# Five feed-forward parts whose rows and weights start at other remainders modulo 128 bytes in SBUF

## The chip, the cores and the metric

The kernel runs on 1 core of one Trainium2 chip, as one launch. The metric is the device time of that core in microseconds (us). The kernel before was timed twice.

## The reference, cut to what matters

The reference is a network of 1024 features and 512 tokens, in float32. Its layers hold five feed-forward parts (two around a recurrent mixer, two around a spatial gating mixer, one behind a last block with attention, a state space branch, a gated linear branch and cross attention). Each part is the same computation with its own weights, here for d = 1024 and f = 2816:

```python
def rms_norm(x, g):
    y = x * rsqrt(mean(x * x, axis=-1) + 1e-6)
    return y * g

def swiglu(x, w_in, w_out):          # w_in [1024, 2*2816], w_out [2816, 1024]
    g, u = split(x @ w_in, 2, axis=-1)
    return (silu(g) * u) @ w_out

h = h + 0.5 * swiglu(rms_norm(h, gain), w_in, w_out)   # four parts; the fifth without the 0.5
```

Between the parts stand the mixers and the last block. The change leaves what they compute and their code as it is, but for the names of the tiles that hold their normed input.

## The kernel before, in words

All arrays are stored with 128 features on the partitions and 512 tokens along the free dimension. A product in float32 is made of three matmuls in the format float32r: every operand is split into a high and a low half (`xg_hi`, `xg_lo` for the rows, `w_hi`, `w_lo` for the weights), and `three_passes` (L457) multiplies high by high, high by low and low by high into one PSUM bank. **Rows** are here the moving operand (the activations, 512 or 256 columns a matmul); **weights** are the stationary operand (128 columns, loaded by a separate LDWEIGHTS).

Weights come from HBM into `w_stage`, a ring of four slots of 1024 float32 each. ScalarE (ACT) writes the high half of a slot into `w_hi` (L424), GpSimd (POOL) the low half into `w_lo` (L448, L455, L803). The loads are issued by the SP queue. Every matrix of the program goes through this ring.

A feed-forward part `i` (`pe_ffn`, L709) has two stages:

- **Up**, with the rows `xg_hi`, `xg_lo` (the normed input). The first and the last pairs of weight slots are multiplied plainly: 8 tiles of the contraction, three passes, 512 columns each (`project_unit`, L464). All between go in **blocks** (`step`, L732): a 2 by 2 block product made with seven products instead of eight. One `step` has seven products of 4 tiles by 3 passes, 84 matmuls of 256 columns (`product`, L712, matmuls at L716 to L718). Three of the seven take their rows from `xg_hi`, `xg_lo` and their weights from the ring (36 matmuls). One takes its rows from `xsum`, sums of rows, and its weights from the ring (12). Three take `xsum` and sums of weights, `s1_w`, `s2_w`, `s3_w` (36). Part 0 has 16 steps, each other part 18.
- **Down**, with the rows `h_hi`, `h_lo` (22 tiles) and the weights from the ring: 8 outputs of 22 tiles by 3 passes, 528 matmuls of 512 columns.

Where a tile lies in SBUF is written by hand. `place` (L149) gives a tile the next free address or the one in `at`. In the kernel before, `x_res`, the ring and all tiles placed after them start at multiples of 2048 bytes, and those placed at `work + n * KB` at multiples of 1024; so the first byte of every high and low half is at remainder 0 modulo 128. The tiles of `k` within them are 2048 bytes apart (1024 in `xsum`), the 128 weight columns of one matmul 512 bytes. One exception matters here: `xsum` lies at `work + 64`, remainder 64. In the notation used below, rows at r and weights at w means the remainders of their start addresses modulo 128.

Order on the engines is fixed by the program text and by semaphores. On TensorE all work of the five parts is in one queue; ACT, DVE and POOL make the sums, the splits and the SwiGLU products beside it.

## Time and profile before

| What | Value |
|---|---|
| Time, median of 2 runs | 2818.24 us (2817.14 and 2819.35) |
| Profiled execution: span, first to last instruction | 2817.5 us |
| TensorE (PE) busy | 2790.9 us, 99% of the span |
| Weight loads (PEld) busy | 2391.3 us, 85% |
| DVE / ACT / POOL busy | 59% / 48% / 56% |
| Mean granted TensorE clock | 0.999 |
| Moved from HBM | 263.09 MB, 94 GB/s |

The page gives the profiled execution's span and no separate time for it. The span lies between the two timed runs, so it is taken as that execution's own time too, and a sum made against it can be held against the median as it is.

How to read the rows: a matmul's duration in the trace (the mean ns of a group) runs from its start until its last result, and neighbours overlap, because matmuls are pipelined. What a matmul costs in a dense stretch is the distance from its start to the start of the next, which is read from a timeline or from a count in a window.

### The profile page before, as it was taken

What the parts mean: (1) busy time and instruction counts of PE and PEld (TensorE: products, weight loads), DVE (VectorE), ACT (ScalarE), POOL (GpSimd) and SP (SyncE); (2) the same over time, 40 slices, a digit from 0 to 9 for tenths busy, and PEclk for the clock granted to TensorE, in tenths of its full rate; (3) what the DMA queues carried; (4) which work ended last, traced back from release to release, by engine and by line L of the source; (5) the groups of instructions that cost most, each with busy time, mean ns of one, the idle gap of its engine ahead of it and who ended that gap; (6) DMA issues with size and microseconds to landing.
All of it is one profiled execution on the core that took longest, in us unless ns stands there. A gap on an engine that the chain in (4) does not pass through costs nothing.

```text
span 2817.5 us, 45558 instructions
## 1 busy us (share of the span) xinstructions
PE 2790.9 (99%) x16386; PEld 2391.3 (85%) x16386; DVE 1657.6 (59%) x2703; ACT 1346.4 (48%) x2076; POOL 1571.1 (56%) x872
## 2 busy tenths in 40 slices
PE   8999999999999999999999999999999999999999
PEld 6998877899889998888999886665688888799987
DVE  6777147677616774135777416579788464477730
ACT  5554257555425554243555334557444444455531
POOL 6775445677547774444777443158633373367743
PEclk9999999999999999999999999999999999999999
DMA  3234322232332233332223332112222342123332
GB/s 136 105 104 115 103 82 82 91 104 104 111 99 90 104 109 105 100 106 89 91 104 120 101 94 77 53 53 66 71 89 70 103 149 75 53 103 107 109 98 77
DMA packets 80685, 267.91 MB, mean 95 GB/s; under 512 B 11168, under 2 KB 13216, under 8 KB 80560
## 3 DMA queue, kind: packets, MB, share of 16 engines
q1 hardware_dynamic: 77904, 262.01, 28.4%
q10 hardware_dynamic: 2656, 4.26, 0.5%
q8 instruction: 74, 1.21, 0.2%
q14 instruction: 51, 0.42, 0.0%
HBM read 263.09 MB, written 2.10 MB: 94 GB/s over the span
## 4 chain that ended last, share of the span: by engine, by line
PE 94%; DVE 3%; ACT 1%; issue 1%; DMA 0%; POOL 0%; ACTq 0%; SPq 0%; DVEq 0%
PE bank L460 17%; PE bank L462 17%; PE bank L461 17%; PE bank L716 10%; PE bank L718 10%; PE bank L717 10%; PE bank L547 1%; PE bank L548 1%; PE bank L549 1%; PE bank L1635 1%; PE bank L2047 1%; PE bank L2915 1%; PE bank L2647 0%; PE bank L2056 0%; PE bank L2627 0%
## 5 line engine op out<-in xcount | busy, mean ns | idle before, releaser
L448 POOL TENSOR_TENSOR w_lo<-w_stage,w_hi 128x1024 fp32r<-128x1024 f32 (+1 forms) x228 | 535.2, 2353 | 714.0 <-ACT w_hi L424 713.5
L424 ACT ACTIVATE w_hi<-w_stage 128x1024 fp32r<-128x1024 f32 (+1 forms) x412 | 421.0, 1027 | 367.2 <-PE bank L462 303.5
L803 POOL TENSOR_TENSOR w_lo<-w_stage,w_hi 128x1024 fp32r<-128x1024 f32 (+1 forms) x176 | 327.3, 1859 | 202.1 <-ACT w_hi L424 202.1
L460 PE MATMUL bank<-xg_hi,w_hi 128*128 128x512 f32 x976 | 396.2, 406 | 5.0 <-DVE h_raw L1063 3.8
L461 PE MATMUL bank<-xg_lo,w_hi 128*128 128x512 f32 x976 | 381.2, 391 | 0.0
L462 PE MATMUL bank<-xg_hi,w_lo 128*128 128x512 f32 x976 | 381.2, 391 | 0.0
L455 POOL TENSOR_TENSOR w_lo<-w_stage,w_hi 128x1024 fp32r<-128x1024 f32 (+1 forms) x96 | 234.9, 2453 | 261.7 <-ACT w_hi L424 217.3
L460 PE MATMUL bank<-h_hi,w_hi 128*128 128x512 f32 x880 | 342.3, 389 | 0.0
L461 PE MATMUL bank<-h_lo,w_hi 128*128 128x512 f32 x880 | 342.3, 389 | 0.0
L462 PE MATMUL bank<-h_hi,w_lo 128*128 128x512 f32 x880 | 342.3, 389 | 0.0
L718 PE MATMUL bank<-xg_hi,w_lo 128*128 128x256 f32 x1056 | 299.2, 283 | 0.0
L716 PE MATMUL bank<-xg_hi,w_hi 128*128 128x256 f32 x1056 | 298.9, 283 | 0.0
L717 PE MATMUL bank<-xg_lo,w_hi 128*128 128x256 f32 x1056 | 298.8, 283 | 0.0
L716 PE MATMUL bank<-xsum,s_w 128*128 128x256 f32 x1056 | 296.1, 280 | 0.0
L718 PE MATMUL bank<-xsum,s_w 128*128 128x256 f32 x1056 | 294.6, 279 | 0.0
L717 PE MATMUL bank<-xsum,s_w 128*128 128x256 f32 x1056 | 294.6, 279 | 0.0
L1136 DVE SCALAR_TENSOR_TENSOR x_res<-bank,x_res 128x512 f32 x64 | 44.0, 687 | 400.9 <-PE bank L462 400.9
L460 PEld LDWEIGHTS bank<-xg_hi,w_hi 128*128 128x128 f32 x976 | 183.6, 188 | 72.5 <-issue 34.5
L1028 DVE TENSOR_TENSOR s_w<-bank,s_w 128x512 fp32r<-128x512 f32 x176 | 121.7, 691 | 190.4 <-ACT s_w L933 190.4
L461 PEld LDWEIGHTS bank<-xg_lo,w_hi 128*128 128x128 f32 x976 | 183.9, 188 | 40.5 <-issue 4.8
L462 PEld LDWEIGHTS bank<-xg_hi,w_lo 128*128 128x128 f32 x976 | 183.6, 188 | 39.7
L716 PEld LDWEIGHTS bank<-xg_hi,w_hi 128*128 128x128 f32 x1056 | 202.4, 192 | 0.2
(530 smaller groups left out, 6599.0 us busy)
## 6 DMA issues: line engine op xcount, KB each, us to landing
w_stage<-w_up SPq DMA_DIRECT2D x220, 512.0 KB, 4.2
w_stage<-w_down SPq DMA_DIRECT2D x80, 512.0 KB, 3.5
w_stage<-merge SPq DMA_DIRECT2D x36, 512.0 KB, 3.4
w_stage<-w_down SPq DMA_DIRECT2D x40, 384.0 KB, 3.2
...
```

What stands on the lines that cost most here:

```text
L424: act.activation(w_hi[:, r, 0:w], w_stage[:, r, 0:w], ACT.Copy).then_inc(w_hi_ready, 1)
L448: pool.tensor_tensor(w_lo[:, r, 0:w], w_stage[:, r, 0:w], f32(w_hi[:, r, 0:w]), ALU.subtract).then_inc(w_lo_ready, 1)
L455: pool.tensor_tensor(w_lo[:, r, 0:w], w_stage[:, r, 0:w], f32(w_hi[:, r, 0:w]), ALU.subtract).then_inc(w_lo_ready, 1)
L460: pe.matmul(out, w_hi[:, r, c], hi, start=start, stop=False)
L461: pe.matmul(out, w_hi[:, r, c], lo, start=False, stop=False)
L462: return pe.matmul(out, w_lo[:, r, c], hi, start=False, stop=stop)
L716: pe.matmul(out, wh[:, c], xh[:, k, :], start=k == 0, stop=False)
L717: pe.matmul(out, wh[:, c], xl[:, k, :], start=False, stop=False)
L718: mm = pe.matmul(out, wl[:, c], xh[:, k, :], start=False, stop=k == 3)
L803: pool.tensor_tensor(w_lo[:, r, cs], w_stage[:, r, cs], f32(w_hi[:, r, cs]), ALU.subtract).then_inc(w_lo_ready, 1)
L1028: dve.tensor_tensor(lo, src[:], f32(hi), ALU.subtract).then_inc(wsum_lo_ready, 1)
L1136: dve.scalar_tensor_tensor(tile(x, m), bank[mm % 4][:], scale, tile(x, m), ALU.mult, ALU.add).then_inc(taken, 1)
```

## The change

The change gives tiles of the same contents several homes, and each feed-forward part uses its own:

- `xg_of[q]`: the normed rows, a pair of tiles for each norm `q`, all over the same memory. `xg_lo` moves 128 bytes further from `xg_hi`.
- The ring: each slot of `w_hi` and `w_lo` gets 32 more float32, so a slot is 4224 bytes long and no longer 4096. The block products of part `i` use columns that begin `BLOCK_ASIDE[i]` float32 into the slot, its down stage `DOWN_ASIDE[i]`. All else, the plain products of the up stage included, begins at the slot's start. Slot r therefore starts 128 * r bytes later than in a ring of 4096.
- `xsum_of`, `s12_of`, `s3_of`, `h_of`, `h_raw_of`: the same for the sums and for `h`. The low half of `h` moves 128 bytes further.
- The size given for dynamic DMA scratch in SBUF is set to 1024, which frees room; the layout is up to some 8 KB longer.

In remainders modulo 128 bytes, rows and then weights (before: 0, 0 everywhere, but for `xsum` with 64, 0):

| Part | blocks, `xg` | blocks, `xsum` | down | plain products of up |
|---|---|---|---|---|
| 0 | 0, 64 | 0, 64 | 64, 64 | 0, 0 |
| 1 | 32, 96 | 32, 96 | 32, 32 | 32, 0 |
| 2 | 96, 32 | 96, 32 | 96, 96 | 96, 0 |
| 3 | 0, 32 | 0, 32 | 0, 32 | 0, 0 |
| 4 | 0, 96 | 0, 96 | 0, 96 | 0, 0 |

No instruction is added, taken out or moved: each of the five engines has the same operations in the same order, with the same waits, and only addresses differ. Its core:

```diff
+    XG_REMAINDER = {0: (0, 0), 1: (0, 0), 2: (32, 32), 3: (96, 96), 4: (0, 0), 5: (0, 0), FINAL: (0, 0), 8: (0, 0), 9: (0, 0)}
+    XSUM_REMAINDER = (0, 32, 96, 0, 0)
+    H_REMAINDER = ((64, 64), (32, 32), (96, 96), (0, 0), (0, 0))
+    BLOCK_ASIDE = (16, 24, 8, 8, 24)
+    DOWN_ASIDE = (16, 8, 24, 8, 24)
...
-    xg_hi = place("xg_hi", [P, KD, T], F32R)
-    xg_lo = place("xg_lo", [P, KD, T], F32R)
+    XG_BASE = cursor[0]
+    xg_of = {q: (place(f"xg_hi{q}", [P, KD, T], F32R, at=XG_BASE + high),
+                 place(f"xg_lo{q}", [P, KD, T], F32R, at=XG_BASE + KD * T * 4 + 128 + low)) for q, (high, low) in XG_REMAINDER.items()}
+    cursor[0] += 2 * KD * T * 4 + LINE
     w_stage = place("w_stage", [P, RING, UNIT])
-    w_hi = place("w_hi", [P, RING, UNIT], F32R)
-    w_lo = place("w_lo", [P, RING, UNIT], F32R)
+    ring_hi = place("ring_hi", [P, RING, UNIT + 32], F32R)
+    ring_lo = place("ring_lo", [P, RING, UNIT + 32], F32R)
+    w_hi, w_lo = ring_hi[:, :, 0:UNIT], ring_lo[:, :, 0:UNIT]
+    wb_of = [(ring_hi[:, :, a:a + UNIT], ring_lo[:, :, a:a + UNIT]) for a in BLOCK_ASIDE]
+    wd_of = [(ring_hi[:, :, a:a + UNIT], ring_lo[:, :, a:a + UNIT]) for a in DOWN_ASIDE]
+
+    def ring_of(L):
+        return wd_of[int(L.name[4])] if L.name.startswith("down") else (w_hi, w_lo)
...
-    h_hi = place("h_hi", [P, KF, T], F32R)
-    h_lo = place("h_lo", [P, KF, T], F32R)
+    h_of = [(place(f"h_hi{i}", [P, KF, T], F32R, at=work + high),
+             place(f"h_lo{i}", [P, KF, T], F32R, at=work + KF * T * 4 + 128 + low)) for i, (high, low) in enumerate(H_REMAINDER)]
...
-    xsum = place("xsum", [P, 4, 2, 4, HALF], F32R, at=work + 64)
-    s1_w = place("s1_w", [P, 2, T], F32R, at=work + 33 * KB)
-    s2_w = place("s2_w", [P, 2, T], F32R, at=work + 37 * KB)
+    xsum_of = [place(f"xsum{i}", [P, 4, 2, 4, HALF], F32R, at=work + off) for i, off in enumerate(XSUM_REMAINDER)]
+    s12_of = [(place(f"s1_w{i}", [P, 2, T], F32R, at=work + 32 * KB + 128 + 4 * a),
+               place(f"s2_w{i}", [P, 2, T], F32R, at=work + 36 * KB + 256 + 4 * a)) for i, a in enumerate(BLOCK_ASIDE)]
...
-    def three_passes(pe, out, r, j, hi, lo, start, stop):
+    def three_passes(pe, out, r, j, hi, lo, start, stop, ring=(w_hi, w_lo)):
 
         c = slice(j * P, (j + 1) * P)
-        pe.matmul(out, w_hi[:, r, c], hi, start=start, stop=False)
-        pe.matmul(out, w_hi[:, r, c], lo, start=False, stop=False)
-        return pe.matmul(out, w_lo[:, r, c], hi, start=False, stop=stop)
+        pe.matmul(out, ring[0][:, r, c], hi, start=start, stop=False)
+        pe.matmul(out, ring[0][:, r, c], lo, start=False, stop=False)
+        return pe.matmul(out, ring[1][:, r, c], hi, start=False, stop=stop)
...
     def pe_ffn(pe, i, q):
+        (s1_w, s2_w), s3_w, (wb_hi, wb_lo) = s12_of[i], s3_of[i], wb_of[i]
         U, L = layers[f"up{i}"], layers[f"down{i}"]
+        xg_hi, xg_lo = xg_of[q]
+        h_hi, h_lo = h_of[i]
+        xsum = xsum_of[i]
...
         def w_block(p, row, c):
             cs = slice(c * T, (c + 1) * T)
-            return w_hi[:, 2 * p + row, cs], w_lo[:, 2 * p + row, cs]
+            return wb_hi[:, 2 * p + row, cs], wb_lo[:, 2 * p + row, cs]
...
-                                          k == 0, k == KF - 1)
+                                          k == 0, k == KF - 1, ring_of(L))
```

The other edits pass the same tiles to ACT, DVE and POOL, which write them.

## Rows read from the trace of the kernel before

**Rows 1.** the page, parts 1 and 2: busy time; slices of the span.
```profile
PE 2790.9 (99%) x16386; PEld 2391.3 (85%) x16386; DVE 1657.6 (59%) x2703; ACT 1346.4 (48%) x2076; POOL 1571.1 (56%) x872
...
PEclk9999999999999999999999999999999999999999
```

**Rows 2.** the page, part 4: the chain that ended last.
```profile
PE 94%; DVE 3%; ACT 1%; issue 1%; DMA 0%; POOL 0%; ACTq 0%; SPq 0%; DVEq 0%
PE bank L460 17%; PE bank L462 17%; PE bank L461 17%; PE bank L716 10%; PE bank L718 10%; PE bank L717 10%; PE bank L547 1%; PE bank L548 1%; PE bank L549 1%; PE bank L1635 1%; PE bank L2047 1%; PE bank L2915 1%; PE bank L2647 0%; PE bank L2056 0%; PE bank L2627 0%
```

**Rows 3.** timeline of PE, one step of part 0: start us, us, engine line op names.
```profile
151.18 0.29 PE L716 MATMUL bank<-xg_hi,w_hi 128*128 128x256 f32 x1
...
155.50 0.28 PE L716 MATMUL bank<-xsum,s_w 128*128 128x256 f32 x1
...
161.16 0.29 PE L716 MATMUL bank<-xg_hi,w_hi 128*128 128x256 f32 x1
```

**Rows 4.** groups by form, PE: names, shapes, count, busy us, mean ns, idle before.
```profile
L716 PE MATMUL bank<-xg_hi,w_hi 128*128 128x256 f32 x1056 | 298.9, 283 | 0.0
...
L716 PE MATMUL bank<-xsum,s_w 128*128 128x256 f32 x1056 | 296.1, 280 | 0.0
...
L716 PE MATMUL bank<-xsum,w_hi 128*128 128x256 f32 x352 | 98.5, 280 | 0.0
```

**Rows 5.** groups by form, weight loads (PEld).
```profile
L716 PEld LDWEIGHTS bank<-xg_hi,w_hi 128*128 128x128 f32 x1056 | 202.4, 192 | 0.2
...
L716 PEld LDWEIGHTS bank<-xsum,s_w 128*128 128x128 f32 x1056 | 198.6, 188 | 0.3
...
L460 PEld LDWEIGHTS bank<-h_hi,w_hi 128*128 128x128 f32 x880 | 165.2, 188 | 34.2
```

**Rows 6.** timeline of PE, projection of the memory: 24 matmuls from first to last row.
```profile
2249.17 0.28 PE L460 MATMUL bank<-mem_hi,w_hi 128*128 128x256 f32 x1
...
2252.04 0.28 PE L460 MATMUL bank<-mem_hi,w_hi 128*128 128x256 f32 x1
```

**Rows 7.** windows: PE, PEld, DVE, ACT, POOL busy (instructions), clock, DMA share, GB/s.
```profile
101.00:211.00 110.00, 110.00 (x928) 110.00 (x927) 82.70 (x155) 59.74 (x100) 82.01 (x56) 1.00 0.30 105
248.00:358.00 110.00, 110.00 (x487) 91.09 (x486) 30.22 (x64) 31.76 (x39) 50.88 (x23) 1.00 0.35 103
```

**Rows 8.** timeline of PE, the forget gate, weights 8 columns wide.
```profile
1718.44 0.39 PE L1683 MATMUL bank<-xg_hi,ff_hi 128*8 128x512 f32 x1
...
1719.12 0.40 PE L1683 MATMUL bank<-xg_hi,ff_hi 128*8 128x512 f32 x1
1719.35 0.40 PE L1684 MATMUL bank<-xg_lo,ff_hi 128*8 128x512 f32 x1
1719.59 0.39 PE L1685 MATMUL bank<-xg_hi,ff_lo 128*8 128x512 f32 x1
...
1723.28 0.40 PE L1683 MATMUL bank<-xg_hi,ff_hi 128*8 128x512 f32 x1
```

**Rows 9.** timeline of PE, down stage of part 0: twelve matmuls from first to last row.
```profile
300.03 0.39 PE L460 MATMUL bank<-h_hi,w_hi 128*128 128x512 f32 x1
...
302.75 0.39 PE L460 MATMUL bank<-h_hi,w_hi 128*128 128x512 f32 x1
```

**Rows 10.** groups by form, ACT: a write at remainder 0, one at 64.
```profile
L424 ACT ACTIVATE w_hi<-w_stage 128x1024 fp32r<-128x1024 f32 x368 | 385.1, 1051 | 234.4 <-PE bank L462 170.7 <-PE bank L549 30.7 <-PE bank L718 24.3
...
L871 ACT ACTIVATE xsum<-xsum_f 128x1024 fp32r<-128x1024 f32 x20 | 20.0, 1047 | 0.2
```

**Rows 11.** groups by form, POOL: the same pair.
```profile
L448 POOL TENSOR_TENSOR w_lo<-w_stage,w_hi 128x1024 fp32r<-128x1024 f32 x188 | 460.4, 2454 | 594.1 <-ACT w_hi L424 593.5
...
L807 POOL TENSOR_TENSOR xsum<-xsum_f,xsum 128x1024 fp32r<-128x1024 f32 x20 | 48.6, 2430 | 0.0
```

**Rows 12.** groups by form, PE: down stage, and projections of the other layers.
```profile
L460 PE MATMUL bank<-xg_hi,w_hi 128*128 128x512 f32 x976 | 396.2, 406 | 5.0 <-DVE h_raw L1063 3.8 <-POOL w_lo L455 1.2
...
L460 PE MATMUL bank<-h_hi,w_hi 128*128 128x512 f32 x880 | 342.3, 389 | 0.0
```

More of the change, by code:

```diff
@@ L173, in build @@
     s3_w = place("s3_w", [P, 2, T], F32R, at=cursor[0] - 2 * T * 4)
+    s3_of = [place(f"s3_w{i}", [P, 2, T], F32R, at=cursor[0] - 2 * T * 4 + 4 * a) for i, a in enumerate(BLOCK_ASIDE)]
+    cursor[0] += LINE
     ss = place("ss", [P, T])
@@ L186, in build @@
     KB = 1024
-    h_raw = place("h_raw", [P, KF, T], at=work + KF * T * 4)
-    xsum = place("xsum", [P, 4, 2, 4, HALF], F32R, at=work + 64)
-    s1_w = place("s1_w", [P, 2, T], F32R, at=work + 33 * KB)
-    s2_w = place("s2_w", [P, 2, T], F32R, at=work + 37 * KB)
+    h_raw_of = [place(f"h_raw{i}", [P, KF, T], at=work + KF * T * 4 + 128 + low) for i, (_, low) in enumerate(H_REMAINDER)]
+    xsum_of = [place(f"xsum{i}", [P, 4, 2, 4, HALF], F32R, at=work + off) for i, off in enumerate(XSUM_REMAINDER)]
+    s12_of = [(place(f"s1_w{i}", [P, 2, T], F32R, at=work + 32 * KB + 128 + 4 * a),
+               place(f"s2_w{i}", [P, 2, T], F32R, at=work + 36 * KB + 256 + 4 * a)) for i, a in enumerate(BLOCK_ASIDE)]
     u_add0 = place("u_add0", [P, T], at=work + 41 * KB)
@@ L423, in split_hi @@
             act.wait_ge(unit_used, b * L.per + (L.base + i + 1 - RING))
-        act.activation(w_hi[:, r, 0:w], w_stage[:, r, 0:w], ACT.Copy).then_inc(w_hi_ready, 1)
+        act.activation(ring_of(L)[0][:, r, 0:w], w_stage[:, r, 0:w], ACT.Copy).then_inc(w_hi_ready, 1)
     def act_bodies(act, L, work=None, only=None):
@@ L447, in body @@
                 pool.wait_ge(w_hi_ready, b * L.per + (L.base + i + 1))
-                pool.tensor_tensor(w_lo[:, r, 0:w], w_stage[:, r, 0:w], f32(w_hi[:, r, 0:w]),
+                hi, lo = ring_of(L)
+                pool.tensor_tensor(lo[:, r, 0:w], w_stage[:, r, 0:w], f32(hi[:, r, 0:w]),
                                    ALU.subtract).then_inc(w_lo_ready, 1)
@@ L566, in act_norm_tile @@
     def act_norm_tile(act, q, gain, m, buf):
-        act.activation(tile(xg_hi, m), tile(x, m), ACT.Copy, scale=col(*gain(m))).then_inc(xg_hi_ready, 1)
+        act.activation(tile(xg_of[q][0], m), tile(x, m), ACT.Copy, scale=col(*gain(m))).then_inc(xg_hi_ready, 1)
         act_norm_square(act, q, m, buf)
@@ L792, in pool_up @@
     def pool_up(pool, U, i):
+        xsum = xsum_of[i]
+        (s1_w, s2_w), s3_w, (wb_hi, wb_lo) = s12_of[i], s3_of[i], wb_of[i]
         def plain(b, u):
@@ L870, in act_x_high @@
         act.wait_ge(xsum_done, XSUMS * i + XSUM_COUNT[t])
-        act.activation(xsum[:, t, 0], xsum_f[:, 1 + t], ACT.Copy).then_inc(wsum_hi_ready, 1)
+        act.activation(xsum_of[i][:, t, 0], xsum_f[:, 1 + t], ACT.Copy).then_inc(wsum_hi_ready, 1)
     def act_ffn_entry(act, i, gain):
@@ L900, in act_ffn @@
     def act_ffn(act, i, gain):
+        h_hi, h_raw = h_of[i][0], h_raw_of[i]
+        (s1_w, s2_w), s3_w, (wb_hi, wb_lo) = s12_of[i], s3_of[i], wb_of[i]
         U, L = layers[f"up{i}"], layers[f"down{i}"]
         def row1(b, p):
-            split_hi(act, U, b, 2 * p)
+            r = 2 * p
+            act.wait_ge(w_loaded[r], b * 16 + 16 * (U.base // RING + 1))
+            act.wait_ge(unit_used, b * 4 + (U.base + r + 1 - RING))
+            act.activation(wb_hi[:, r, :], w_stage[:, r, :], ACT.Copy).then_inc(w_hi_ready, 1)
         def row2(b, p):
@@ L909, in row2 @@
             act.wait_ge(unit_used, b * 4 + (U.base + r + 1 - RING))
-            act.activation(w_hi[:, r, T:2 * T], w_stage[:, r, T:2 * T], ACT.Copy).then_inc(w_hi_ready, 1)
+            act.activation(wb_hi[:, r, T:2 * T], w_stage[:, r, T:2 * T], ACT.Copy).then_inc(w_hi_ready, 1)
         def copy21(b, p, n):
@@ L1236, in pe_rec @@
                 pe.wait_ge(gates_sig, 2 * KD)
-            project_unit(pe, R if s < KD else Y, u // 4, u % 4, xg_hi, xg_lo,
+            project_unit(pe, R if s < KD else Y, u // 4, u % 4, *xg_of[q],
                          (xg_lo_ready, split_count(q)) if s == 0 else None, out=y_bank(u) if s >= KD else None)
@@ L1377, in norms_read @@
             pe.wait_ge(col_std, 1)
-        pe_project_tokens(pe, V, xg_hi, xg_lo, norm=norms, ready=(xg_lo_ready, split_count(q)), between=norms_read)
+        pe_project_tokens(pe, V, *xg_of[q], norm=norms, ready=(xg_lo_ready, split_count(q)), between=norms_read)
         def mix(h):
@@ L1390, in pe_sgu @@
         for u in range(KD):
-            project_unit(pe, U, u // 4, u % 4, xg_hi, xg_lo, free=V.rbase + u + 1 if u < 4 else None)
+            project_unit(pe, U, u // 4, u % 4, *xg_of[q], free=V.rbase + u + 1 if u < 4 else None)
             if u == 2:
@@ L1527, in result @@
                 act.wait_ge(taken, m + (L.rbase + 1))
-                act.activation(tile(xg_hi, m), tile(x, m), ACT.Copy, scale=gain12[:, bass.ds(m, 1)]).then_inc(xg_hi_ready, 1)
+                act.activation(tile(xg_of[FINAL][0], m), tile(x, m), ACT.Copy, scale=gain12[:, bass.ds(m, 1)]).then_inc(xg_hi_ready, 1)
                 act.wait_ge(ss_added, m * 2 + ((KD + 1) * FINAL + 2))
@@ L2019, in first_half @@
             half(u, 0)
+        xg_hi, xg_lo = xg_of[FINAL]
         def half(u, part):
@@ L3262, in _ @@
             act.wait_ge(x_in[m // 2], 32)
-            act.activation(xg_hi[:, m, :], x[:, m, :], ACT.Copy, scale=col("ffn1_norm", m)).then_inc(xg_hi_ready, 1)
+            act.activation(xg_of[0][0][:, m, :], x[:, m, :], ACT.Copy, scale=col("ffn1_norm", m)).then_inc(xg_hi_ready, 1)
         split_hi(act, order[0], 0, 1)
```

20 lines of the change are left out of this document (15 added, 5 removed).

## The prediction

> **What bounds the kernel now.** I read the page's first parts first. TensorE (PE) is busy for 2790.9 of 2817.5 us, and its granted clock is at the upper of its two levels, 2.4 GHz, in all slices [rows 1]. The chain that ended last agrees: 94% of it is matmuls, over half of it the 512-column passes of L460 to L462 and 30% the block products of L716 to L718 [rows 2]. So the time is a number of matmuls times the distance from one start to the next, and a change of addresses matters to the end only through that distance, as long as no other engine becomes late.
>
> Then the distances. At 2.4 GHz a matmul of 256 columns streams in 106.7 ns and one of 512 in 213.3 ns. In a step of part 0, the 36 matmuls on `xg` take 155.50 - 151.18 = 4.32 us, **120.0 ns each**; the 48 matmuls on `xsum` behind them take 161.16 - 155.50 = 5.66 us, **117.9 ns each** [rows 3]. The down stage goes at 2.72 us / 12 = **226.7 ns** each [rows 9]; its group has one mean, 389 ns, over all five parts [rows 12], so I take 226.7 for each of them. All of these are 11 to 13 ns above the streaming time.
>
> Why are `xsum` products 2.1 ns faster? The groups show the same shape and form, 283 against 280 ns [rows 4]. The weights are not the reason: `xsum` with weights from the ring has the same 280 ns as with the sums [rows 4]. The steps between tiles are not the reason either: the memory's rows have tiles 1024 bytes apart like `xsum`, but start at remainder 0, and go at 2.87 us / 24 = 119.6 ns [rows 6], the pace of `xg`. What is left is the start: `xsum` is the only one of the three at remainder 64, with its weights at 0. The weight loads tell the same: 192 ns beside rows at 0, 188 ns beside `xsum` [rows 5]. I read it as this: a load and a stream that begin at the same remainder disturb each other by some 4 ns, of which half shows in the distance. With 512 columns the load has twice the time.
>
> **The change part by part.** No instruction comes or goes; five things move.
>
> 1. *Blocks of parts 0 to 2, rows on `xg`.* Rows and weights come to stand 64 apart (0 and 64, 32 and 96, 96 and 32), where they were 0 apart. Steps: 16 + 18 + 18 = 52, of 36 such matmuls, 1872 in all. At 120.0 - 117.9 = 2.1 ns each that is **-3.9 us**. That the distance modulo 128 decides, and not both remainders by themselves, is an assumption; the rows have only 0 with 0 and 64 with 0.
> 2. *Blocks of parts 0 to 2, rows on `xsum`.* 64 apart before and after: **0**.
> 3. *Blocks of parts 3 and 4.* All pairs are now 32 or 96 apart, which no row shows. 36 steps: 1296 matmuls on `xg` (now 120.0) and 1728 on `xsum` (now 117.9). Bounds: all of them at 117.9 gives -1296 x 2.1 = -2.7 us; all at 120.0 gives +1728 x 2.1 = +3.6 us. I take the middle, 118.95 ns for both, since 32 lies between 0 and 64: -1.4 + 1.8 = **+0.4 us**. The far ends are in the rivals.
> 4. *Down stages.* Parts 0 to 2 keep rows and weights together (64, 32, 96): by the assumption of step 1, 0. Parts 3 and 4 have 1056 matmuls with the weights alone at 32 or 96. The nearest row with such weights is the forget gate, whose weights are 8 columns (32 bytes) a tile, so that they start at 0, 32, 64, 96, 128 and so on, with rows at 0. Its first three passes take 0.68 us, 226.7 each; the next 18 take 4.16 us, 231.1 each [rows 8], so +4.4 ns. But these loads are 8 columns wide, not 128. On the other side stands a gain like that of the blocks, -2.1 ns. Between +4.6 and -2.2 us I take **0**: in a down stage a load is recorded with 188 ns like the undisturbed ones [rows 5] beside a matmul of 389 [rows 12], so it has time to spare, and the blocks' 2.1 ns need not show there.
> 5. *Everything else.* The plain products of parts 1 and 2 have rows at 32 and 96 against weights at 0: 2 x 192 = 384 matmuls, 0 in the middle, between -0.8 and +1.7 us by the prices of step 4. The low halves are 128 bytes further and slot r of the ring 128 * r bytes; modulo 128 nothing changes, so 0 (but see the second rival). Sum without the rivals: -3.9 + 0 + 0.4 + 0 + 0 = -3.5 us.
>
> *Cover.* The other engines now read and write at 32, 64 and 96. At 64 that is free: ACT needs 1047 ns into `xsum` and 1051 into the ring for the same size [rows 10], POOL 2430 and 2454 [rows 11]. For 32 and 96 there is no row. In the blocks DVE is busy for 82.7, POOL for 82.0 and ACT for 59.7 of 110 us, and PE for all 110 with 928 matmuls; in the down stage they have at most 50.9 of 110 [rows 7]. A tenth more on all of them would leave POOL at 90 of 110 and PE still ahead. If that cover went, PE's idle time before L716, 0.0 us now [rows 4], would grow, by DVE's and POOL's low halves first, the two with the least room. Should PE get faster by 2% the same room holds. The DMAs land in `w_stage`, whose slots stay as they are.
>
> 2817.5 - 3.5 = 2814.0 us for the profiled execution. Its span lies between the two timed runs, and the median is 0.7 us above it; I predict **2814 us**.
>
> **The rivals.**
>
> *Nothing moves (2818 us).* The `xsum` products are faster for a reason that moves with them, such as what precedes them in the queue. For it: only 2.1 ns are at stake, and no two rows differ in the remainder alone. Against it: the memory's rows. The time is that of before, 2817.5 to 2818. The Trainium skill ("SBUF — State Buffer", Specifications) gives 16-byte cachelines to SBUF as the unit whose crossing costs; 32, 64 and 96 all start such a line, and so by that rule no start here is worse or better than another. The difference between 283 and 280 ns [rows 4] speaks against the rule being the whole story.
>
> *Slower: weights that do not start at a multiple of 256 bytes.* In the forget gate the tile at 128 goes no faster than those at 32 or 96: the 18 passes that take 231.1 each hold it [rows 8]. If it is the weights' start and not their width, the price of 4.4 ns is paid by every 512-column pass whose weights are off such a start. These are all 2640 of the down stages (+11.6 us), and, since slots 1 and 3 of the longer ring now start 128 bytes off, half of the passes of all other projections. L460 to L462 have 976 such groups of three on `xg` alone [rows 12], so about 2930 passes, of which half pay: +6.4 us. With -3.5 us from the forecast's steps this makes 2817.5 + 11.6 + 6.4 - 3.5 = **2832 us**. It decides from the point where the down stage of any part goes above 228 ns; if only weights alone at 32 or 96 pay (parts 3 and 4), it is +4.6 us and 2818.6. Against it: 8-column loads are the only such row, and weights at 0 never show it in a dense stretch.
>
> *More is gained: another distance lets the passes close up.* The 11 to 13 ns above streaming are there in each pass, and nothing in the rows says that 0 and 64 are the only levels. The lower bound is streaming itself. In the down stages of parts 3 and 4 that is -1056 x 13.4 = -14.1 us, **2800 us** with the forecast's -3.5; if the blocks of these parts close up too, another -1296 x 13.3 - 1728 x 11.2 = -36.6 us, 2763 us. For it: 64 apart already took 2.1 ns. Against it: it took only 2.1 of 13.3, and the 8-column loads, which hardly read anything, do not come below 226.7 either [rows 8], so most of the gap does not come from the load beside. The Trainium skill ("TensorE: Matmul & The Clock Gate", Wait — 56ns, not 53.3ns?) gives N / 2.4 + 2.5 ns from start to start for bfloat16; that would be 215.8 ns for 512 columns, and by it the most that the two down stages could gain is 11.5 us. The trace has 226.7 in float32r and no row of it shows that pace.
>
> *The change does not do what it says.* The remainders come from absolute offsets that I worked out from the listing; the base of all is rounded to 128, then to 2048 bytes, in both kernels, so a shift against the table is hardly possible. I give it no share of its own.
>
> **How the numbers follow.** Forecast, 2808 to 2817: 0.50. Nothing moves: 0.17. Slower, 2818.6 to 2832 and somewhat above: 0.18. More is gained, 2763 to 2807: 0.15. The range reaches from the first half of the third rival, 2800, to the full price of the second, 2832, with 2 us on either side for the spread of the runs: **2798 to 2834**; outside are some 0.10 below and 0.06 above. Two per cent, taken as what a measurement of this kernel can tell from no change, is 56 us. Faster by that would need 2762, the whole of the third rival and a little more: 0.03. Slower by that would need 5.5 ns on all of the some 10,000 matmuls of the five parts, 1.2 times the gate's price even where only 256 columns are streamed: 0.02. Within: 0.95.
>
> **What would show it.** In the trace of the changed kernel: (1) start to start of the `xg` block matmuls in parts 0 to 2 at about 117.9 ns, and their weight loads at 188 in place of 192 ns; that fails if they stay at 120. (2) The `xsum` matmuls there unchanged. (3) In parts 3 and 4 both kinds between 117.9 and 120. (4) The down stages at 226.7 in all five parts; above 228 is the second rival, below 222 the third. (5) The projections outside the five parts as before; if they slow down, the ring's longer slots are the cause. (6) PE's idle time before L716's successor still 0. The prediction is wrong in kind if the five parts differ from each other by more than 2 ns a matmul, and if DVE, ACT or POOL appear as what PE waits for.

## The result, and the profile after

The changed kernel takes **2836.56 us** (2835.99 and 2837.13), against 2818.24: a ratio of 1.006, with a 95% interval of 1.0041 to 1.0079. It is slower by 18 us. My 2814 was wrong in sign, and 2836.6 lies above the range, which ended at 2834.

The first parts of the page and the share by engine of the chain that ended last:

```profile
span 2835.3 us, 45558 instructions
...
PE 2809.5 (99%) x16386; PEld 2383.4 (84%) x16386; DVE 1658.5 (58%) x2703; ACT 1345.1 (47%) x2076; POOL 1572.8 (55%) x872
...
PEclk9999999999999999999999999999999999999999
...
PE 95%; DVE 3%; ACT 1%; issue 1%; DMA 0%; POOL 0%; ACTq 0%; SPq 0%; DVEq 0%
```

Against [rows 1, 2] one thing moves: PE is busy 18.6 us longer with the same 16386 matmuls, at the upper clock level in every slice. No other engine's busy time moves by more than 1.7 us, and none is waited for more by over 0.3 us. So what changed is the distance from start to start, and that is what the rest of this text reads. Below it stands for five places of the timeline of PE after: one step of part 0 (answers [rows 3]), the down stage of part 0 and that of part 3, first and last of 528 matmuls each ([rows 9]), and in the layer with rows `m`, which the change did not touch, 21 matmuls in an even slot of the ring and 21 in the odd slot behind it.

```profile
141.00 0.28 PE L739 MATMUL bank<-xg_hi,ring_hi 128*128 128x256 f32 x1
...
145.24 0.28 PE L739 MATMUL bank<-xsum,s_w 128*128 128x256 f32 x1
...
150.80 0.28 PE L739 MATMUL bank<-xg_hi,ring_hi 128*128 128x256 f32 x1
...
243.00 0.39 PE L478 MATMUL bank<-h_hi,ring_hi 128*128 128x512 f32 x1
...
364.77 0.39 PE L480 MATMUL bank<-h_hi,ring_lo 128*128 128x512 f32 x1
...
1570.24 0.40 PE L478 MATMUL bank<-h_hi,ring_hi 128*128 128x512 f32 x1
...
1692.67 0.40 PE L480 MATMUL bank<-h_hi,ring_lo 128*128 128x512 f32 x1
...
2333.77 0.39 PE L478 MATMUL bank<-m_hi,ring_hi 128*128 128x512 f32 x1
...
2338.30 0.40 PE L480 MATMUL bank<-m_hi,ring_lo 128*128 128x512 f32 x1
...
2339.24 0.39 PE L478 MATMUL bank<-m_hi,ring_hi 128*128 128x512 f32 x1
...
2343.89 0.40 PE L480 MATMUL bank<-m_hi,ring_lo 128*128 128x512 f32 x1
```

The block products got faster: 36 on `xg` in 4.24 us, 117.8 ns each, and 48 on `xsum` in 5.56 us, 115.8 ns. The down stages got slower: 121.77 us / 527 = 231.1 ns in part 0, 122.43 / 527 = 232.3 in part 3, where each had 226.7. The layer on `m` is at 4.53 us / 20 = 226.5 ns in the even slot, as before, and at 4.65 / 20 = 232.5 in the odd one. The odd slots begin 128 bytes off a multiple of 256.

Within the down stage of part 0 the two kinds of slot differ the other way round. Its rows are at 64 (high) and 192 (low) modulo 256, its weights at 64 in an even slot and at 192 in an odd one. Three starts, of an even slot with 24 matmuls, an odd one with 18 and the next even one:

```profile
263.69 0.40 PE L478 MATMUL bank<-h_hi,ring_hi 128*128 128x512 f32 x1
...
269.30 0.39 PE L478 MATMUL bank<-h_hi,ring_hi 128*128 128x512 f32 x1
...
273.42 0.40 PE L478 MATMUL bank<-h_hi,ring_hi 128*128 128x512 f32 x1
```

The even slot takes 5.61 us / 24 = 233.8 ns a matmul, the odd one 4.12 / 18 = 228.9. The other slots of this stage have the same two paces, but for the first one, which is even and goes at 229.2.

The groups by form (PE, then weight loads) answer [rows 4, 5, 12]: the load beside `xg` fell from 192 to 188 ns, as forecast, and no idle time came before the block products. The mean of 188 is over all five parts. The window of the blocks holds 945 matmuls in 110 us where there were 928 ([rows 7]).

```profile
L478 PE MATMUL bank<-h_hi,ring_hi 128*128 128x512 f32 x880 | 347.0, 394 | 0.0
...
L739 PE MATMUL bank<-xg_hi,ring_hi 128*128 128x256 f32 x1056 | 296.0, 280 | 0.0
...
L739 PE MATMUL bank<-xsum,s_w 128*128 128x256 f32 x1056 | 294.8, 279 | 0.0
```

```profile
L739 PEld LDWEIGHTS bank<-xg_hi,ring_hi 128*128 128x128 f32 x1056 | 198.4, 188 | 0.2
```

```profile
101.00:211.00 110.00, 110.00 (x945) 110.00 (x944) 84.04 (x157) 59.91 (x102) 83.98 (x58) 1.00 0.30 105
```

The table has this account for every kernel here: the block stages and the down stages of the five parts, each from the start of its first matmul to that of its last, summed, and the rest up to the start of the program's last matmul. The rest holds the other layers, the plain products of the up stages, and the program's start: the first block stage begins 61.1 to 64.5 us into the span, 62.8 before and 64.0 in the change. In that start the granted clock falls to its lower level, 1.2 GHz, for 3.4 us before (from 39.9 us on) and for 6.8 in the change (from 38.3 on). Between 30 and 40 us TensorE was busy for 6.2 and 5.9 of 10 us there; in b1_xglow, where it was busy for 7.4, the clock did not fall. So 1 to 3 us of a difference in the rest can be the start alone.

| Kernel | blocks, us | down, us | rest, us | time, us |
|---|---|---|---|---|
| before | 877.7 | 597.3 | 1338.9 | 2818.2 |
| the change | 868.3 | 610.3 | 1353.1 | 2836.6 |
| a1_slots | 862.0 | 606.3 | 1349.0 | 2822.8 |
| a2_lows | 853.7 | 609.0 | 1350.0 | 2818.1 |
| a3_by256 | 870.4 | 604.9 | 1342.0 | 2822.8 |
| a4_rows0_w64 | 867.9 | 597.3 | 1340.4 | 2811.0 |
| b1_xglow | 853.5 | 597.3 | 1341.3 | 2799.7 |
| b2_map | 864.4 | 606.2 | 1341.5 | 2817.6 |
| c1_xglow192 | 854.2 | 597.5 | 1340.2 | 2797.5 |
| c2_xglow64 | 871.6 | 597.3 | 1344.5 | 2820.7 |
| c3_part1 | 873.0 | 597.3 | 1341.1 | 2816.8 |
| d1_lowmap | 869.4 | 597.4 | 1342.6 | 2814.9 |
| d2_summap | 873.5 | 597.3 | 1341.6 | 2817.9 |

So the change is worth -9.4 us in the blocks, +13.0 in the down stages and +14.2 elsewhere. The times of before, the change, a4, b1, c1 and c2 are medians of several runs, the others one run each; the three columns of stages are always from the one profiled execution. The kernel before, run again beside the experiments, took 2818.5 to 2825.9 us, so a single time is good only to some us. The stages repeat better: the down stages are at 597.3 to 597.5 us in seven of the experiments.

### The profile page after: what moved, and what is told of

Its sections match the earlier page's. It is cut to its first block, busy times and chain, and to the rows that moved or that the text cites. A ratio compares the mean times of both kernels' runs of the same rounds, so it can differ in the third digit from the quotient of the medians.

```text
span 2835.3 us, 45558 instructions
## 1 busy us (share of the span) xinstructions
PE 2809.5 (99%) x16386; PEld 2383.4 (84%) x16386; DVE 1658.5 (58%) x2703; ACT 1345.1 (47%) x2076; POOL 1572.8 (55%) x872
## 4 chain that ended last, share of the span: by engine, by line
PE 95%; DVE 3%; ACT 1%; issue 1%; DMA 0%; POOL 0%; ACTq 0%; SPq 0%; DVEq 0%
PE bank L478 18%; PE bank L480 18%; PE bank L479 18%; PE bank L741 10%; PE bank L740 10%; PE bank L739 10%; PE bank L565 1%; PE bank L566 1%; PE bank L567 1%; PE bank L1669 1%; PE bank L2084 1%; PE bank L2954 1%; PE bank L2686 0%; PE bank L2093 0%; PE bank L2666 0%
## 5 line engine op out<-in xcount | busy, mean ns | idle before, releaser
L466 POOL TENSOR_TENSOR ring_lo<-w_stage,ring_hi 128x1024 fp32r<-128x1024 f32 (+1 forms) x228 | 537.4, 2363 | 732.3 <-ACT ring_hi L441 732.0
L441 ACT ACTIVATE ring_hi<-w_stage 128x1024 fp32r<-128x1024 f32 (+1 forms) x324 | 328.7, 1021 | 377.2 <-PE bank L480 310.8
L828 POOL TENSOR_TENSOR ring_lo<-w_stage,ring_hi 128x1024 fp32r<-128x1024 f32 (+1 forms) x176 | 327.0, 1858 | 197.5 <-ACT ring_hi L934 197.0
L478 PE MATMUL bank<-xg_hi,ring_hi 128*128 128x512 f32 x976 | 400.3, 410 | 5.2 <-DVE h_raw L1095 4.1
L480 PE MATMUL bank<-xg_hi,ring_lo 128*128 128x512 f32 x976 | 384.4, 394 | 0.0
L479 PE MATMUL bank<-xg_lo,ring_hi 128*128 128x512 f32 x976 | 383.6, 393 | 0.0
L473 POOL TENSOR_TENSOR ring_lo<-w_stage,ring_hi 128x1024 fp32r<-128x1024 f32 (+1 forms) x96 | 234.9, 2452 | 263.5 <-ACT ring_hi L441 218.6
L478 PE MATMUL bank<-h_hi,ring_hi 128*128 128x512 f32 x880 | 347.0, 394 | 0.0
L479 PE MATMUL bank<-h_lo,ring_hi 128*128 128x512 f32 x880 | 345.8, 393 | 0.0
L480 PE MATMUL bank<-h_hi,ring_lo 128*128 128x512 f32 x880 | 345.8, 393 | 0.0
L741 PE MATMUL bank<-xg_hi,ring_lo 128*128 128x256 f32 x1056 | 296.2, 281 | 0.0
L480 PEld LDWEIGHTS bank<-xg_hi,ring_lo 128*128 128x128 f32 x976 | 183.7, 188 | 43.9
L741 PEld LDWEIGHTS bank<-xg_hi,ring_lo 128*128 128x128 f32 x1056 | 199.1, 189 | 0.0
```

Source lines behind the costliest of these rows:

```text
L441: act.activation(ring_of(L)[0][:, r, 0:w], w_stage[:, r, 0:w], ACT.Copy).then_inc(w_hi_ready, 1)
L466: pool.tensor_tensor(lo[:, r, 0:w], w_stage[:, r, 0:w], f32(hi[:, r, 0:w]), ALU.subtract).then_inc(w_lo_ready, 1)
L473: pool.tensor_tensor(w_lo[:, r, 0:w], w_stage[:, r, 0:w], f32(w_hi[:, r, 0:w]), ALU.subtract).then_inc(w_lo_ready, 1)
L478: pe.matmul(out, ring[0][:, r, c], hi, start=start, stop=False)
L479: pe.matmul(out, ring[0][:, r, c], lo, start=False, stop=False)
L480: return pe.matmul(out, ring[1][:, r, c], hi, start=False, stop=stop)
```

## The experiments

All are cut from the changed kernel by its tables and its two fixed steps: the padding of a ring slot (32 float32) and of the low halves (128 bytes). The change has a third, `s1_w` 128 bytes off a multiple of 256. In a3, a4 and b2 the 128 is made 256, and in all other experiments `s1_w` is back where it was before, so its share in the blocks of the change was not measured by itself. The longer layout stays in all of them. "All homes 0" means the tables as before: rows and weights at 0, `xsum` at 64.

**Which of the two fixed steps costs, and where?** Both kernels have all homes 0.

```diff
 # a1_slots
-    ... at=XG_BASE + KD * T * 4 + 128 + low        # xg_lo; the same for h_lo
+    ... at=XG_BASE + KD * T * 4 + 0 + low
     ring_hi = place("ring_hi", [P, RING, UNIT + 32], F32R)
 # a2_lows
     ... at=XG_BASE + KD * T * 4 + 128 + low
-    ring_hi = place("ring_hi", [P, RING, UNIT + 32], F32R)
+    ring_hi = place("ring_hi", [P, RING, UNIT + 0], F32R)
```

> Of the change only the longer ring: slots of 4224 bytes, so that slot r starts 128 * r bytes later; rows, low halves and sums as in the kernel before. Theory 256 (what counts is the distance of rows and weights modulo 256): every 512-column pass with its weights in slot 1 or 3 goes from 226.7 to about 232.5 ns, those in slots 0 and 2 stay; the down stages go from 119.5 to about 121.0 us each, the other projections slow down likewise, and the span rises by some 15 us to about 2832 us, less what blocks gain or lose. Rival theory 128 (only the remainder modulo 128 counts, and the other layers slowed down for another reason, such as the shifted layout): 226.7 everywhere and a span of 2817 to 2819 us.

> Of the change only the low halves of xg and h, 128 bytes further; ring and sums as in the kernel before. Theory 256: only passes on xg_lo and h_lo, and their neighbours, change; the down stages and the projections on xg go from 226.7 to 228 to 233 ns, the projections whose rows are neither (sgy, yh, m, o) stay at 226.7 in all slots. Blocks on xg get faster by one or two ns or stay, blocks on xsum stay at 117.9. Span 2820 to 2830 us. Rival theory 128: nothing moves, 2817 to 2819 us.

Measured: 2822.8 and 2818.1 us; the kernel before had a median of 2820.3 beside them (2818.45 to 2823.46). Down stage of part 0, first and last of 528, of a1_slots:

```profile
241.83 0.39 PE L478 MATMUL bank<-h_hi,ring_hi 128*128 128x512 f32 x1
...
363.10 0.40 PE L480 MATMUL bank<-h_hi,ring_lo 128*128 128x512 f32 x1
```

and of a2_lows, with one step of its blocks ahead:

```profile
140.67 0.28 PE L739 MATMUL bank<-xg_hi,ring_hi 128*128 128x256 f32 x1
...
144.91 0.28 PE L739 MATMUL bank<-xsum,s_w 128*128 128x256 f32 x1
...
150.35 0.28 PE L739 MATMUL bank<-xg_hi,ring_hi 128*128 128x256 f32 x1
...
241.70 0.40 PE L478 MATMUL bank<-h_hi,ring_hi 128*128 128x512 f32 x1
...
363.50 0.39 PE L480 MATMUL bank<-h_hi,ring_lo 128*128 128x512 f32 x1
```

Of the 2.3 us that the down stage of part 0 lost, the slots alone cost 1.8 (121.27 us, 230.1 ns a matmul) and the low halves alone 2.35 (121.80 us, 231.1 ns). The slots slow the odd slots of all layers (`m`: 226.5 and 232.5 ns, as in the changed kernel); the low halves leave `m` alone. And each makes the blocks faster. In a2_lows the sums go at 5.44 us / 48 = **113.3 ns**, although no address of a product on sums was touched. That pace stands in no row of before, and its cause cannot be the addresses of that product alone. In a1_slots too the products on `xsum` and sums of weights have their old addresses, and two of the three run at 113.3 ns there, the third at 117.9. By the table the blocks gain 15.7 us in a1_slots and 24.0 in a2_lows. The expectation for a1 had left the blocks open; that for a2 had put the sums at 117.9 ns, and its 2820 to 2830 us was too high for that reason.

**Is it the distance modulo 256?** The change with both fixed steps made 256 bytes, all its homes kept.

```diff
-    ... + KD * T * 4 + 128 + low      /  UNIT + 32
+    ... + KD * T * 4 + 256 + low      /  UNIT + 64
```

> The change with all its homes, but every step of 128 made one of 256: low halves 256 bytes further, slots of 4352 bytes, sums at multiples of 256 plus the part's remainder. Theory 256: all projections outside the five parts are back at 226.7 ns, the down stages of parts 0 to 2 too (rows and weights together), so 119.5 us each; the blocks on xg and xsum of parts 0 and 1 (rows 64 below the weights) go at 113.3 ns, those of part 2 (rows 96, weights 32) at 117.5. Span about 2817.5 - 21 (blocks of parts 0, 1: some 16 to 18; part 2 and the others 2 to 5) = 2795 to 2802 us, if the down stages of parts 3 and 4 lose no more than 3 us each. Rival theory 128: as the changed kernel, 2835 us, with 231 ns in the down stages.

Measured: 2822.8 us. Down stages of part 0 (rows and weights at 64) and of part 4 (0 and 96), first and last:

```profile
243.63 0.39 PE L478 MATMUL bank<-h_hi,ring_hi 128*128 128x512 f32 x1
...
363.13 0.39 PE L480 MATMUL bank<-h_hi,ring_lo 128*128 128x512 f32 x1
...
2693.85 0.39 PE L478 MATMUL bank<-h_hi,ring_hi 128*128 128x512 f32 x1
...
2817.32 0.40 PE L480 MATMUL bank<-h_hi,ring_lo 128*128 128x512 f32 x1
```

Part 0 is back at 226.7 ns, and so are the down stages of parts 1 and 2 and the other layers (`m`: 227.1 ns in the mean). Part 4 is at 234.3, part 3 at 233.3. So a 512-column pass costs 226.7 ns where rows and weights begin together modulo 256, whatever the remainder is. The expectation for the blocks failed, and with it the span of 2795 to 2802 us: they stayed between 117.4 and 118.5 ns. The shifted layout is not a cause of its own, since the other layers are back with it in place. And without the padding the change still does not gain: by the table its stages sum to 3.4 us more than before, where the forecast was 3.5 less.

**Rows at 0 against all weights at 64.**

```diff
-    XSUM_REMAINDER = (64, 64, 64, 64, 64)      BLOCK_ASIDE = (0, 0, 0, 0, 0)
+    XSUM_REMAINDER = (0, 0, 0, 0, 0)           BLOCK_ASIDE = (16, 16, 16, 16, 16)
```

(from all homes 0, low halves not moved, slots of 4352 bytes, sums of weights at 64)

> One home for all five parts: all rows at 0 modulo 256, xsum too; the weights of the blocks and the sums of weights at 64 modulo 256 (slots of 4352 bytes), the weights of down stages, plain products and all other layers at 0 modulo 256. Theory 256: all 7392 block matmuls go at 113.3 ns and all else stays as in the kernel before: 3168 x 6.7 + 4224 x 4.6 = 21.2 + 19.4 = 40.6 us less than 2818, so about 2777 us. Rival theory 128: the blocks go at 117.9 (rows 64 away from weights, the sign does not count), 3168 x 2.1 = 6.7 us less, 2811 us.

Measured: 2811.0 us (2807.8 to 2812.9), ratio 0.9965, interval 0.9951 to 0.998. Four starts of a step in part 1, 84 matmuls each:

```profile
593.44 0.28 PE L739 MATMUL bank<-xg_hi,ring_hi 128*128 128x256 f32 x1
602.99 0.28 PE L739 MATMUL bank<-xg_hi,ring_hi 128*128 128x256 f32 x1
612.86 0.28 PE L739 MATMUL bank<-xg_hi,ring_hi 128*128 128x256 f32 x1
622.75 0.28 PE L739 MATMUL bank<-xg_hi,ring_hi 128*128 128x256 f32 x1
```

The first step takes 9.55 us, 113.7 ns a matmul; the next two 9.87 and 9.89, 117.5 and 117.7, with every address the same and the granted clock at its upper level throughout. **One set of addresses has at least two steady paces.** The expected time supposed the fast one throughout; the slow one won in all of parts 0, 2 and 3. Part 1 ran five of its 18 steps at 113.7 to 114.6 ns and part 4 three at 113.8 to 114.5, and both fell back.

**Only the helpful half of the change.** The kernel before with the low half of the norm's rows 128 bytes off, in the five parts alone.

```diff
-    XG_REMAINDER = {0: (0, 0), 1: (0, 0), 2: (0, 0), 3: (0, 0), 4: (0, 0), 5: (0, 0), ...
+    XG_REMAINDER = {0: (0, 128), 1: (0, 0), 2: (0, 128), 3: (0, 128), 4: (0, 0), 5: (0, 128), ...
```

> The kernel before with one edit: in the five feed-forward parts xg_lo lies 128 bytes further (remainder 128 modulo 256); ring, h, sums and all other layers stay. New theory (two paces, kept from what ran before): a block product on xsum, whose own addresses are untouched, runs at 113.3 ns instead of 117.8 once the xg products before it have broken the slow pace, and the xg products run at 117.8; block stages 174.6 us instead of 179.5 (155.2 instead of 159.6 in part 0), together -24 us; the 960 plain passes of the up stages pay 4.4 ns each, +4.2 us; down stages 119.5 us each as before. Total about 2818 - 20 = 2798 us. Rival (the pace is a function of a product's own two addresses alone): xsum stays at 117.8 and only xg gains, 3168 x 2.2 = 7.0 us, less 4.2: 2815 us.

Measured: **2799.7 us** (2797.6 to 2800.8), ratio 0.9922, interval 0.9904 to 0.9939. One step of part 1:

```profile
606.47 0.28 PE L739 MATMUL bank<-xg_hi,ring_hi 128*128 128x256 f32 x1
...
610.71 0.28 PE L739 MATMUL bank<-xsum,s_w 128*128 128x256 f32 x1
...
616.15 0.28 PE L739 MATMUL bank<-xg_hi,ring_hi 128*128 128x256 f32 x1
```

117.8 ns on `xg`, 113.3 on `xsum`: the blocks give 24.2 us, the down stages stay at 597.3, and only the plain products of the up stages pay: 231 to 233 ns, which for 960 of them at 4.4 ns or more is an estimated 4 us; the rest as a whole is 2.4 us longer, with a start that is 1.3 us shorter. The kernel before had 2818.7 to 2825.5 us beside it.

**A map of further distances.** Each part has its own pair; slots of 4352 bytes.

```diff
+    XG_REMAINDER = {0: (64, 192), 2: (64, 64), 3: (0, 128), 5: (0, 128), 9: (64, 192), others (0, 0)}
+    XSUM_REMAINDER = (64, 64, 128, 192, 192)    H_REMAINDER = ((0, 0), (0, 0), (0, 0), (128, 128), (64, 64))
+    BLOCK_ASIDE = (0, 0, 16, 0, 0)              DOWN_ASIDE = (16, 32, 48, 32, 0)
```

> A map: each part has other homes modulo 256 (slots of 4352 bytes, sums at multiples of 256 plus the blocks' weights). Blocks, rows xg high and low, rows xsum, weights: part 0 64/192, 64, 0; part 1 64/64, 64, 0; part 2 0/128, 128, 64; part 3 0/128, 192, 0; part 4 64/192, 192, 0. Down, rows and weights: 0, 64; 0, 128; 0, 192; 128, 128; 64, 0. Two-pace theory: part 1 stays at 117.8 on both kinds, since nothing breaks the slow pace; parts with the low half 128 apart reach 113.3 at least on xsum. Theory 256 for 512 columns: the down stage of part 3 (together at 128) goes at 226.7 ns, 119.5 us; parts 0, 1, 2 and 4 (64, 128, 192 apart) go at 231 to 234 ns, 121.8 to 123.4 us. Rival for 512 columns (64 apart is good, as in the blocks): parts 0 and 4, or 2, go at 224 ns or less. Projections outside the parts at 226.7.

Measured: 2817.6 us. Down stage of part 2, rows 0 and weights 192:

```profile
1082.03 0.39 PE L478 MATMUL bank<-h_hi,ring_hi 128*128 128x512 f32 x1
...
1202.66 0.39 PE L480 MATMUL bank<-h_hi,ring_lo 128*128 128x512 f32 x1
```

120.63 us / 527 = 228.9 ns. Part 4, rows 64 and weights 0, the same distance of 192, has 228.9 too. No distance was better than 0, so the rival for 512 columns fell. For the blocks the two-pace theory failed in part: the low half was 128 bytes from the high one, modulo 256, in four parts, but the sums ran at 113.5 ns in part 3 alone; they stayed at 117.8 in parts 0 and 2, and in part 4 they alternated between 113.3 and 117.8 from step to step.

With a3_by256 this gives the price list of a 512-column pass, by weights minus rows modulo 256, both halves alike:

| Distance | 0 | 32 | 64 | 96 | 128 | 160 | 192 | 224 |
|---|---|---|---|---|---|---|---|---|
| ns | 226.7 | 233.3 | 233.3 | 234.3 | 232.4 | 233.3 | 228.9 | 233.3 |

0 is five pairs (0, 32, 64, 96 and 128 on both sides); 160 and 224 are the plain products of parts 2 and 1 of a3_by256 (rows 96 and 32, weights 0).

**Which displacement of the low half?**

```diff
-    XG_REMAINDER = {0: (0, 128), ...
+    XG_REMAINDER = {0: (0, 192), ...      # c1_xglow192, all five parts
+    XG_REMAINDER = {0: (0, 64), ...       # c2_xglow64, all five parts
+    XG_REMAINDER = {2: (0, 128), ...      # c3_part1, part 1 alone
```

> As b1_xglow (the kernel before, with the low halves of the norm's rows displaced in the five parts), but by 192 bytes in place of 128. Theory: the price of a 512-column pass is read by the distance of rows and weights modulo 256, and 192 costs some 2 ns (228.7 in the down stage of part 2 of b2_map) where 128 costs 4 to 6; the block products only ask that the distance is not 0. Then the blocks stay at 174.6 us (113.3 ns for the products on sums), the plain projections of the parts fall from 231 to 232 ns a pass to about 229, and the time is about 2797. Rival: the pace of 113.3 ns needs exactly 128 between the halves; then the sums go back to 117.8 ns, the blocks take 178 us each and the time is about 2813.

> As b1_xglow, with the low halves displaced by 64 bytes. Theory: 64 costs a 512-column pass most (233.3 ns in the down stage of part 0 of b2_map), the blocks as with 128: plain projections at 231 to 233 ns, blocks 174.6 us, time 2800. Rival as for c1_xglow192: without exactly 128 between the halves the sums stay at 117.8 ns, time about 2816.

> The kernel before, with the low halves of the norm's rows displaced by 128 bytes in part 1 alone. Theory: the pace of the products on sums follows the products just before them in the same step, so that it is local: blocks of part 1 174.6 us with sums at 113.3 ns from the third step on, blocks of the other four parts as before (159.6, 179.4 to 179.6 us), time some 4 us below the kernel before. Rival: the fast pace stays once it is entered, so that parts 2, 3 and 4 also run their sums at 113.3 ns (their blocks at about 176 us), time some 14 us below.

Measured: c1 **2797.5 us** (2796.9 to 2804.0), ratio 0.9928, interval 0.9912 to 0.9945; c2 2820.7, ratio 1.0003, interval 0.9993 to 1.0012; c3 2816.8. Plain products of part 1 in c1, 42 matmuls from first to last row:

```profile
712.08 0.39 PE L478 MATMUL bank<-xg_hi,ring_hi 128*128 128x512 f32 x1
...
721.69 0.39 PE L478 MATMUL bank<-xg_hi,ring_hi 128*128 128x512 f32 x1
```

That is 228.8 ns, as the price list has for 192. A step of part 0 in c2:

```profile
141.74 0.28 PE L739 MATMUL bank<-xg_hi,ring_hi 128*128 128x256 f32 x1
...
145.97 0.28 PE L739 MATMUL bank<-xsum,s_w 128*128 128x256 f32 x1
...
151.62 0.28 PE L739 MATMUL bank<-xg_hi,ring_hi 128*128 128x256 f32 x1
```

117.5 and 117.7 ns: at 64 the rival came true and the sums stayed slow. (Nor does 64 cost a 512-column pass most: 96 does in the price list.) A step of part 1 of the same run, where every remainder is that of part 0:

```profile
623.79 0.28 PE L739 MATMUL bank<-xg_hi,ring_hi 128*128 128x256 f32 x1
...
628.10 0.28 PE L739 MATMUL bank<-xsum,s_w 128*128 128x256 f32 x1
...
633.76 0.28 PE L739 MATMUL bank<-xg_hi,ring_hi 128*128 128x256 f32 x1
```

Here `xg` goes at 4.31 us / 36 = 119.7 ns, as it does in part 2, and at 117.6 in parts 3 and 4: a second case of one set of remainders with two steady paces. And a step of part 2 in c3, behind the displaced part 1 (whose blocks took 174.6 us):

```profile
954.59 0.29 PE L739 MATMUL bank<-xg_hi,ring_hi 128*128 128x256 f32 x1
...
958.91 0.28 PE L739 MATMUL bank<-xsum,s_w 128*128 128x256 f32 x1
...
964.57 0.29 PE L739 MATMUL bank<-xg_hi,ring_hi 128*128 128x256 f32 x1
```

120.0 and 117.9 ns, as in [rows 3]. Only `xg_lo` of one part differs between c3 and the kernel before, in remainders, so here the fast pace of the sums comes with the displaced `xg` products ahead of them, and ends with them. The third step of part 1 is the first with the fast sums.

**Is there a rule for the fast pace?**

```diff
+    XG_REMAINDER = {0: (0, 32), 2: (0, 96), 3: (0, 160), 5: (0, 224), 9: (128, 192), ...      # d1_lowmap
+    XG_REMAINDER = {0: (0, 128), ...      XSUM_REMAINDER = (0, 32, 96, 128, 160)              # d2_summap
```

> The kernel before, with the low halves of the norm's rows at 32, 96, 160 and 224 bytes in parts 0 to 3 (high halves at 0), and high 128, low 192 in part 4. So far low halves at 128 and 192 let the products on sums fall to 113.3 ns, and at 64 they don't. Theory: what counts is a distance of 128 or more modulo 256: parts 0 and 1 as before or as with 64 (blocks 157.8 to 159.6 and 177.7 to 179.6 us, sums 117.8 ns), parts 2 and 3 blocks 174.6 us with sums at 113.3 ns, part 4 the same; time about 2806. Rival: only whole steps of 64 from 128 on do it; then parts 2 and 3 stay at 177.7 to 179.6 us too, and the time is about 2815. The plain projections of the part tell a third thing: by the down stages of the runs so far a distance of 160 or 224 costs a 512-column pass as much as 32 or 96, 230 to 234 ns.

> As b1_xglow (low halves of the norm's rows at 128 in the five parts), with the sums' rows at 0, 32, 96, 128 and 160 bytes in parts 0 to 4 in place of 64. Theory: the products on sums go at 113.3 ns when they are behind such xg products and their own distance is not 0. Then part 0 (distance 0) goes back to 117.8 to 120 ns on sums (blocks 159 us), parts 1 to 4 stay at 174.6 us; time about 2804. Rival: the distance of the sums' rows does not matter once the pace is entered; then part 0 is at 155 us too and the time is 2800.

Measured: 2814.9 and 2817.9 us. A step of part 1 in d1 (low half at 96):

```profile
611.05 0.28 PE L739 MATMUL bank<-xg_hi,ring_hi 128*128 128x256 f32 x1
...
615.28 0.28 PE L739 MATMUL bank<-xsum,s_w 128*128 128x256 f32 x1
...
620.73 0.28 PE L739 MATMUL bank<-xg_hi,ring_hi 128*128 128x256 f32 x1
```

The sums go at 5.45 us / 48 = 113.5 ns there, and at 117.6 to 117.9 in the other four parts. Both theories of d1 fell. With the high half and the weights at 0 and the sums at 64, a low half at 96, 128 or 192 gives the fast pace; at 32, 64, 160 and 224 it does not. Nor does part 4, high half at 128 and low at 192. The plain products of parts 2 and 3 (low half at 160 and 224) take 231 to 233 ns, as was expected. In d2 the sums take 120.0, 116.8, 119.9, 119.1 and 117.5 ns with their rows at 0, 32, 96, 128 and 160, so both expectations for d2 fell too, but for part 0, where the theory was right. Of the starts tried behind such `xg` products only 64 (b1) and 192 (113.5 ns, part 3 of b2_map) are fast.

## Why the prediction was wrong

**The step that failed** is one half sentence of step 5, "modulo 128 nothing changes, so 0", resting on the assumption of step 1 that the distance modulo 128 decides. The trace of before had no pair 128 apart in a long row of passes, and I took the remainder modulo 128 from the way the change is written. The period is 256: 128 apart costs 5.7 ns in a 512-column pass, nearly as much as 32 or 64 (6.6), and 256 apart costs nothing (a3_by256). With it, both fixed steps, which the forecast passed over as bookkeeping, became the largest terms: 14.4 us between the change and a3_by256 by the table.

**A second step failed by itself.** Step 4 put the weights of parts 3 and 4 at 0, on the argument that a load has time to spare beside 512 columns. Without any fixed step these down stages still lose 3.5 and 4.0 us (a3_by256), and the plain products of parts 1 and 2, which step 5 put at 0 in the middle, go at 233.3 ns, which is an estimated 2.5 us for 384 of them. It is the 512-column pass that pays. So even without padding the change would have been about 3 us slower, and the sign of the forecast wrong.

- *Step 1* (-3.9 us): the size was about right. `xg` in parts 0 to 2 is at 117.5 to 117.8 ns, and the loads of all parts at 188. 64 apart is enough for it, since a3_by256 has 117.8 in part 0 with no other step; but it is not needed, since a2_lows has 117.8 too, with the high half and the weights still together.
- *Step 2* (0): sums at 115.9, 115.9 and 117.5 ns in parts 0 to 2, where 117.9 was expected; without the fixed steps they are at 117.6 to 117.8 (a3_by256), so the step as such was right. In parts 0 and 1 one of four products on sums runs at 113.3. Part 3 has 119.0, 3.1 ns more than parts 0 and 1, so the sign that I had given for being wrong in kind, over 2 ns between the parts, was met.
- *Step 3* (+0.4): parts 3 and 4 gave 0.4 and 0.8 us back. With steps 1 and 2 the blocks gave 9.4 us, not 3.5.
- *Step 4* (0): +13.0 us. Parts 0 to 2, where I had cost an edit at 0, lost 2.3 us each, all from the two fixed steps: a3_by256, without them, has 119.5 us there. Parts 3 and 4 lost 3.0 and 3.1, less than without the fixed steps.
- *Step 5* (0): +14.2 us, of which 1.2 lie ahead of the first block stage. a1_slots and a2_lows have +10 and +11 alone, so the two do not add up. The down stage of part 0 shows how: in an odd slot the low rows and the weights, both 128 further, stand together again, and the pace there is 228.9 ns, where a1_slots has 232.8.
- *Cover* held: no idle time came before the blocks, and no engine but PE is busy longer by more than 0.2%.
- *The base.* In every run here the time of an execution is 1.8 to 1.9 us above its span (2837.13 and 2835.3 us for the change). The span of 2817.5 was therefore not that execution's own time, as I took it, and the forecast of 2814.0 was a span, or 2815.8 us of time. That changes nothing in the sign. The 5.5 ns of the last estimate were for 10,000 matmuls; the parts have 10,992, so it is 5.1.

**The rivals.** "Weights that do not start at a multiple of 256 bytes" was nearly right, in mechanism and in price (4.4 ns from the forget gate; the down stages now pay 4.4 to 5.8). It named the odd slots, and "above 228 is the second rival" was met by all five down stages. Two things it missed: the low halves pay in the same way, and what counts is the distance, not the weights' own start, since weights at 128 with rows at 128 take 226.7 ns (part 3 of b2_map). Its terms came out at 13.0 us for its 11.6 and 14.2 for its 6.4, which counted the projections on `xg` alone and not those of the other layers (`m`, `sgy`, `yh`, `o`, `y`: 1104 passes), and the blocks gave 9.4 us back, not 3.5. The row that bore on it was there, read, and given 0.18 because its loads are 8 columns wide. "More is gained" existed as well, in the blocks, but not in the down stages of parts 3 and 4, where it looked first. "Nothing moves" fell in its time; its reason, that what precedes the `xsum` products sets their pace, is in part what c3_part1 shows. The page beside it, "SBUF — State Buffer" of the Trainium skill, section Specifications, prices a crossing of 16-byte lines; every start here is on such a line, and the paces range from 226.7 to 234.3 ns. The same page of the Trainium skill, section A bandwidth-pool intuition that's wrong (but worth ruling out), lists a second independent read port for LDWEIGHTS. If that is read as saying that rows and weights never disturb each other, the price list above goes against it.

**What stays open.** Why the block products have three paces (120.0, 117.8, 113.3 ns), and which of them a given set of addresses takes; means in between, such as 116.8 and 119.1 in d2, are unexplained too. The runs show that the fastest depends on what ran before, not on the products' own addresses alone (a2, a4, c3), that one set of remainders can hold either of two paces (a4, c2), and that it does not follow a threshold in the low half's distance (d1) or need only that the sums are apart from their weights (d2). What links them in the engine no run shows. The price list of the 512-column passes is safe only where both halves are alike: with the low half alone 128 off, a2_lows has 231.1 ns in all down slots and the change 233.8 in an even slot of part 0, at the same distances. Whether a matmul's rows are disturbed by its own weight load or by the next one was not separated.
